# A second layer norm's weights loaded earlier, and turned attention probabilities copied by ScalarE, in a fused three-layer kernel on one Trainium2 core

## The reference, cut to what matters

```python
x = layer_norm(ALPHA * x + gdn_mixer(x, ...), ln_g[0, 0], ln_b[0, 0])   # first norm
x = layer_norm(ALPHA * x + swiglu(x, ...),    ln_g[0, 1], ln_b[0, 1])   # second norm
h = s5_mixer(x, ...)       # its tables depend on weights alone, not on x
...
p = softmax(q @ k.T * scale + bias)   # 8 heads, 256 queries, 256 keys
o = p @ v                             # TensorE wants p with the keys on the partitions: p is turned
```

## Time and profile before

| | |
|---|---|
| median of 3 runs | 1318.15 us (1315.19, 1318.15, 1319.48) |
| the profiled execution, its own time | 1316.35 us |
| its span, on which the trace's times lie | 1314.5 us |
| mean granted TensorE clock | 0.992 of full speed |
| PE busy | 1265.9 us, 96% of the span |
| DVE / ACT / POOL busy | 44% / 18% / 8% |
| read from and written to HBM | 274.19 MB and 16.78 MB |

### The profile page before, as it was taken

The page is one execution under the profiler, slowest core; times in us unless marked ns, Lnnn a source line. Parts: engine busy times, 40 slices in busy tenths (PEclk is TensorE's granted clock), DMA queues, the critical chain, the costliest instruction groups (busy, mean ns, idle before and its releaser), DMA issues.

```text
span 1314.5 us, 25628 instructions
## 1 busy us (share of the span) xinstructions
PE 1265.9 (96%) x11215; PEld 935.5 (71%) x11215; DVE 572.5 (44%) x1078; ACT 234.6 (18%) x494; POOL 111.6 (8%) x109
## 2 busy tenths in 40 slices
PE   7999999999999979899999999999999979999997
PEld 6888985899974448447577767776746645999443
DVE  0653644576789746424211110111062274555545
ACT  2461341123110102502001010100021021111000
POOL 1036102400001000000200000000133000000000
PEclk9999999999999989998999999999999999999999
DMA  9954120565754661747999999999997240353530
GB/s 342 355 210 115 46 97 0 116 176 149 190 225 168 140 125 34 263 170 281 382 418 417 406 406 418 415 405 406 376 349 229 73 184 0 129 191 136 195 120 32
DMA packets 119820, 292.09 MB, mean 222 GB/s; under 512 B 6268, under 2 KB 66144, under 8 KB 107456
## 3 DMA queue, kind: packets, MB, share of 16 engines
q1 hardware_dynamic: 107584, 270.29, 56.9%
q0 software_dynamic: 4800, 14.67, 3.7%
q10 hardware_dynamic: 7360, 6.03, 1.5%
HBM read 274.19 MB, written 16.78 MB: 221 GB/s over the span
## 4 chain that ended last, share of the span: by engine, by line
PE 90%; DVE 5%; ACT 2%; DMA 1%; issue 1%; POOL 0%; DVEq 0%; ACTq 0%; POOLq 0%
PE bank L2565 18%; PE bank L2343 11%; PE bank L2015 9%; PE bank L2582 9%; PE bank L2737 8%; PE bank L2775 7%; PE bank L2028 6%; PE bank L2350 4%; PE bank L2500 4%; PE bank L1987 3%; PE bank L2426 2%; PE bank L2159 1%; PE bank L2449 1%; PE bank L2145 1%; PE bank L2199 1%
## 5 line engine op out<-in xcount | busy, mean ns | idle before, releaser
L2565 PE MATMUL bank<-arena 128*32 128x352 f32 x3072 | 234.8, 461 | 1.4 <-DVE arena L1360 0.7
L2565 PEld LDWEIGHTS bank<-arena 128*32 128x32 f32 x3072 | 142.5, 110 | 87.6 <-issue 6.7
L2015 PE MATMUL bank<-xT,arena 128*128 128x256 f32 x608 | 133.8, 379 | 2.2 <-ACT arena L1695 1.4
L2015 PEld LDWEIGHTS bank<-xT,arena 128*128 128x128 f32 x608 | 114.4, 190 | 17.9 <-ACT arena L1695 1.8
L2582 PE MATMUL bank<-arena 128*32 128x256 f32 x2112 | 119.3, 379 | 0.0
L2582 PEld LDWEIGHTS bank<-arena 128*32 128x32 f32 x2112 | 108.0, 110 | 8.9
L1405 DVE TENSOR_TENSOR arena<-arena,bank 128x352 f32<-128x352 f32 x24 | 19.3, 805 | 205.7 <-PE bank L2565 205.7
L2775 PE MATMUL bank<-arena 128*128 128x512 f32 x224 | 96.7, 592 | 0.7 <-DVE arena L1537 0.7
L2343 PE MATMUL bank<-xT,arena 128*128 128x128 f32 x704 | 83.1, 275 | 0.0
L2343 PEld LDWEIGHTS bank<-xT,arena 128*128 128x128 f32 x704 | 80.8, 192 | 1.3 <-issue 1.3
L2775 PEld LDWEIGHTS bank<-arena 128*128 128x128 f32 x224 | 42.3, 190 | 53.6 <-issue 49.5
(11 more groups left out here) (424 smaller groups left out, 1499.7 us busy)
## 6 DMA issues: line engine op xcount, KB each, us to landing
arena<-moe_w SPq DMA_DIRECT2D x64, 1408.0 KB, 14.3
arena<-moe_w SPq DMA_DIRECT2D x24, 1536.0 KB, 16.4
arena<-ffn_w SPq DMA_DIRECT2D x44, 512.0 KB, 6.0
arena<-gdn_w_in SPq DMA_DIRECT2D x8, 2048.0 KB, 20.3
arena<-w_up SPq DMA_DIRECT2D x8, 2048.0 KB, 8.9
arena<-w_down SPq DMA_DIRECT2D x8, 2048.0 KB, 7.7
arena<-ffn_w SPq DMA_DIRECT2D x11, 1024.0 KB, 5.2
slot_rows<-arena SPq DMA_DIRECT2D x1, 9600.0 KB, 50.8
```

What stands on the lines that cost most here:

```text
L2015: last = mm(bank[:, at:at + SEQ], w[:, k, P * m:P * m + P], x[:, k, :], start=(k == 0), stop=(k == KT - 1))
L2565: last = mm(banks[i][32 * q:32 * q + 32, 0:EW1], xg[:, t, EK * s + kk], w[:, kk, EW1 * q:EW1 * q + EW1], start=(s == 0 and kk == 0), stop= ...
```

## The change: what it does

- `norm_w` is scratch no longer. `t_p` is replaced by `t_up`, 1024 words in the arena at 28160, for the first `w_tables`, and by `t_down`, which is `xT` seen flat, for all later tables. `f_c21` moves to the arena at 27136. Both arena pieces lie in the tail of `V`, which only `v_tables(2)` and `v_tables(3)` write.
- POOL no longer waits for `v_ready`; it issues the second norm's two loads right behind the router's weights, ahead of `s5_pool`.
- In the attention the two copies into `probT` leave DVE. ACT makes them (`take_turned`): those of head pair hp stand between the exponentials of steps 2 hp + 2 and 2 hp + 3, the last pair's behind all exponentials. From the second pair on they also wait for the product with the values of the pair before (`pv_done`).

```diff
@@ -243,9 +243,9 @@
         tb = region(34784, PAIRS, GC)
         kzero = region(35296, 1024)
 
-        flat_w = norm_w[:].rearrange("p a b -> p (a b)")
-        t_p, t_v = flat_w[:, 0:PIECE * 9 * GC], flat_w[:, PIECE * 9 * GC:PIECE * 9 * GC * 3 // 2]
-        f_c21 = flat_w[:, 1728:1984].rearrange("p (a b) -> p a b", a=2)
+        t_up = region(28160, PIECE * SUB * GC)
+        t_down = xT[:].rearrange("p a b -> p (a b)")[:, 0:PIECE * 9 * GC]
+        f_c21 = region(27136, 2, P)
         d_col = d_small[0:2 * GC]
 
         s5_in_w = [region(o_, 4, DM) for o_ in (0, 4096)]
@@ -720,10 +720,9 @@
 
             pool.wait_ge(norm_done, 4)
             pool.dma_start(w_router, A["moe_w_router"][0].rearrange("(k p) f -> p k f", p=P)).then_inc(small_loaded, 16)
-            s5_pool(pool, link)
-            pool.wait_ge(v_ready, 2 * NPIECE)
             norm_load(0, "ln_g", DM)
             norm_load(1, "ln_b", DM)
+            s5_pool(pool, link)
             for n in (2, 3):
                 pool.wait_ge(norm_done, 4 * n)
                 norm_load(0, "ln_g", n * DM)
@@ -1116,7 +1115,7 @@
                 if j:
                     dve.wait_ge(w_tr, 4 * j)
                 for part in parts:
-                    s5_w_table(V_, link, j, part, t_p).then_inc(w_ready, 1)
+                    s5_w_table(V_, link, j, part, t_down if j else t_up).then_inc(w_ready, 1)
                     dve.wait_ge(w_ready, 2 * j + part + 1)
 
             def s5_pieces(c):
@@ -1222,7 +1221,7 @@
             def v_tables(j):
 
                 for part in range(2):
-                    s5_v_table(V_, link, slice(PIECE * j, PIECE * (j + 1)), part, t_p).then_inc(v_ready, 1)
+                    s5_v_table(V_, link, slice(PIECE * j, PIECE * (j + 1)), part, t_down).then_inc(v_ready, 1)
                     dve.wait_ge(v_ready, 2 * j + part + 1)
 
             def take_kernel(j):
@@ -1505,10 +1504,6 @@
                 V_.tensor_tensor(p, p, total[:, :, None].broadcast_to((P, 2, SEQ)), ALU.mult).then_inc(pn_ready, 1)
                 if n == 0 and hp:
                     head_outputs(hp - 1)
-                if n == 1:
-                    for kt in range(2):
-                        dve.wait_ge(pt_done, 2 * hp + kt + 1)
-                        V_.tensor_copy(probT[:, kt].rearrange("p a b -> p (a b)"), banks[4 + kt][:, :]).then_inc(pt_read, 1)
             head_outputs(3)
 
             def weight_sums(j):
@@ -1930,15 +1925,26 @@
             for m in range(4):
                 act.wait_ge(p_done, 2 + m + 1)
                 A_(q2[:, m], banks[4 + m][:, 0:SEQ], ACT.Copy, scale=AD ** -0.5).then_inc(p_read_a, 1)
+            def take_turned(hp):
+
+                for kt in range(2):
+                    act.wait_ge(pt_done, 2 * hp + kt + 1)
+                    if hp:
+                        act.wait_ge(pv_done, hp)
+                    nc.scalar.copy(probT[:, kt].rearrange("p a b -> p (a b)"), banks[4 + kt][:, :]).then_inc(pt_read, 1)
+
             for hp in range(4):
                 for n in range(NT):
                     i = 2 * hp + n
+                    if n and hp:
+                        take_turned(hp - 1)
                     act.wait_ge(max_ready, i + 1)
                     if hp >= 2:
                         act.wait_ge(pt_done, 2 * (hp - 1))
                     for e in range(2):
                         A_(prob[hp % 2][:, n, e], banks[2 * n + e][:, 0:SEQ], ACT.Exp, bias=nmax[:, n, e:e + 1],
                            accum_out=psum_p[:, n, e:e + 1]).then_inc(exp_done, 1)
+            take_turned(3)
             for n in range(NT):
                 vector_step()
                 mean_square(n)
```

## The result

Five runs of the changed kernel took 1308.39 to 1311.82 us, median 1310.27; five runs of the kernel before took 1315.19 to 1319.98, median 1319.48. The ratio is 0.9943, with a 95% interval of 0.9931 to 0.9956. On the prediction's base of 1317.25 that is 7.5 us less, about 1309.7, where 9.2 less, 1308.0, was forecast. On the same base the interval stands for 5.8 to 9.1 us less: it holds rival B's 7.2 and just leaves out 9.2. So the kernel is faster and the time lies in the range, but the gain is nearer to B's. The trace says that it is B.

A forecast was written before the change was run, and what follows sets the result against it. PE work was taken as the bound, 90% of the chain that ended last. Second norm 9.0 plus attention 0.2, other costs 0, made 9.2 us off 1317.25: forecast 1308.0 us, range 1305.0 to 1312.5.

The forecast's parts named there:

- rival B: Products up: third chunk's weights come 3.6 us late, PE loses 2.0, gain is 7.2 us (1310.0); chance 0.12.
- Part 1: Second norm: earlier weight loads save 9.0 us, from PE's 6.3 stall plus 0.9 (transposes) and 1.8 (matmuls) at half clock.
- Rival A: Second norm: the wait goes but not the whole stretch, so only about 5.5 us is gained (1311.7); chance 0.10.
- The cost of the earlier loads: Products up: 1 MB added beside the third chunk's weights was taken to cost 0, with 2.0 us kept for the range.
- bound from above: Third chunk's weights: 2.5 us transfer plus 1.1 us later issue on POOL, 3.6 us in all; PE would lose 2.0.
- second step: Products up: DVE's work ends 1.6 us before PE wants it, cover to set against the 3.6 us delay.
- The S5 parameters: POOL's S5 loads, now behind the norm loads: 1.1 or 3.6 us later, inside 5 us of cover before ACT; cost 0.
- Rival C: Small S5 loads land 24 us late, PE stands 19 us, net 10 us slower (1327); chance 0.03.
- The scratch: Tables: scratch in `xT` and the arena instead of `norm_w` changes only the address; cost nothing.
- Part 2: Attention: copies moved from DVE to ACT gain 0 in three middle rounds and 0.2 us in the last.
- Shifted whole: S5 and the experts: all that follows the second norm was let move earlier by its full 9.0 us.
- Rival D: A later stage that waits for data alone swallows all of the 9.2 us (1317); chance 0.03.

The follow-up runs named there:

- e1: Kernel before with only the scratch moved, norm loads still waiting for the tables; S5 input product starts 239.24 us behind the first norm's last turn.
- e2: Kernel before with only ACT's copies of the turned probabilities added; ratio 0.9997 (0.9988 to 1.0005), 12 runs.
- run 150: Not a run's number: 150 packets left in the memset run, the kernel with late norm loads plus an early 1.0 us POOL memset; first sum at +20.92 us.
- a1: The changed kernel run again unaltered; median 1312.44 us of six runs, ratio 0.995 against the kernel before.
- e3: Kernel after with the attention of before, so only scratch and norm loads changed; median 1310.46 us of eight runs, ratio 0.9951.
- e8: Kernel after with POOL's four zero stores moved behind `bb_ready`; third chunk's first sum starts 20.75 us behind the first norm's last turn.
- e9: Kernel after with the two `s_d` loads ahead of the norm loads; third chunk's first sum starts 21.59 us behind the first norm's last turn.

## Why the prediction was right, and where it was not

- **Part 1, 9.0 us: right in sum and in its terms.** With the loads out of everybody's way it is 9.09. Tile 0's turn comes 6.47 us earlier (228.07 behind the first norm's turn before, 221.60 with the loads late) where 6.3 was said, and the clock gives back 2.62 where 0.9 + 1.8 was said. Rival A (5.5 us) is out. That the sum fits to 0.1 us is partly luck: prediction and offset both start from one execution of the kernel before. Against e1 and e2, which keep the wait, the gain with the loads late is 8.6 and 7.7 us (239.24 and 238.35 less 230.65), because the reload landed sooner in them; by the times it is 8.6, with an interval of 7.0 to 10.1.
- **The cost of the earlier loads: the step that failed.** "I take 0" was wrong. The bound from above was what happened: 3.41 us of delay where it said 3.6, and 1.96 us of PE's time (232.61 - 230.65) where it said 2.0. So the gain up to S5 was 7.13 us, rival B's 7.2, to which I had given 0.12. The choice rested on a mean, 2.4 us of DMA time free in ten. But what counts is what is under way when the half goes out. And the two terms of my bound are not the mechanism: it added a transfer of 2.5 us and a later issue of 1.1, while the runs show 2.8 us from the later issue by itself, 3.4 with the bytes in front of it, and 4.4 from the bytes with the list issued on time. So the bound came out near by luck. What held is its second step: 3.41 us less the 1.6 of cover leaves PE 1.8, and 1.96 was measured.
- **The S5 parameters, cost 0: right** for those who use them; ACT never waits. What I left out is what those loads, moved, do to somebody else's transfer. Rival C (24 us late) is out: the `s_d` loads landed 7.1 us after issue, not 6.1.
- **The scratch, 0: right** (e1).
- **Part 2, 0.2 us: right.** Rounds of 6.91 us as before, 0.22 in the last one, by the traces; the times cannot show it.
- **Shifted whole: right, as far as it can be seen.** The input product of S5 starts 5.58 us earlier on the trace's own axis (482.91 to 477.33: 7.13 less the 1.55 by which the turn was late), the attention's scores 5.93 (1050.67 to 1044.74), the output product 6.15 (1080.79 to 1074.64), the end 6.1. Rival D is out.
- **The total.** 9.09 - 1.96 + 0.22 = 7.35 us against the 7.5 of the ratio, whose interval is 5.8 to 9.1; with the scatter of the first term, that they agree to 0.15 is luck too.

## What to carry to other kernels

When a load is moved to a place that looks idle, a mean share of the DMA engines does not price it: find the next transfer on the path, look at what is under way at its issue, and count every DMA that the move pushes next to it, not only the one that is moved. If the data is wanted 200 us later, there is a better place than the first free one; here a place 117 us further on gave the 2 us back. And where a wait leaves PE standing, count the half clock behind it as well: here it was 2.6 us on top of 6.5.

## What was unexpected in the hardware

- A memset of 1 us on POOL, ahead of a list of small loads, delays another queue's load of 512 KB by 2.7 us (7.6 to 10.3) though that load is issued at the same moment; two tiny loads in its place give the same 10.3. The DMA queues in the ten microseconds from +10 on, in the memset run and then with the loads late (packets, MB, share of 16 engines' time; q1 is SP's queue, q0 POOL's):

```profile
q1 hardware_dynamic: 2074, 1.05, 59.6%
q0 software_dynamic: 384, 0.80, 39.1%
```

```profile
q1 hardware_dynamic: 2080, 1.05, 57.6%
q0 software_dynamic: 345, 0.76, 31.0%
```

  SP's packets as a whole take hardly more of the engines' time. What is late is their end. With the loads late all 2080 have been moved by +18. In the memset run 150 are left then; these are the next two microseconds, one by one:

```profile
q1 hardware_dynamic: 73, 0.03, 31.3%
```

```profile
q1 hardware_dynamic: 71, 0.03, 11.7%
```

  31.3% and 11.7% of 16 engines are the time of about five and two engines (an estimate from these shares). So the load's landing waits for the packets of a few DMA engines while most have done their part. Why these few are behind is open.
- In the kernel after SP's packets are slow as a whole: in the same ten microseconds its 1.03 MB took 72.5% of 16 engines' time, where 1.05 MB took 54.4% before (71.5%, 71.0% and 73.4% in a1, e3 and e8). With the `s_d` loads first (e9) it is 59.3%, and the sum is as late as ever, so this slowness is not what the delay needs. The kernel after, then before:

```profile
q1 hardware_dynamic: 2033, 1.03, 72.5%
q0 software_dynamic: 382, 0.80, 36.2%
```

```profile
q1 hardware_dynamic: 2080, 1.05, 54.4%
q0 software_dynamic: 345, 0.76, 31.3%
```

- One and the same pair of 512 KB loads landed 10.6 and 12.43 us after issue beside the tables' loads, 5.2 and 6.3 us beside the S5 loads, and 4.1 and 5.3 in the late place. The Trainium skill, DMA: Bandwidth & Descriptors, section Anatomy of one DMA, gives 2.0 us and a rate of 436 GB/s, from which I estimated 3.2 and 4.4 for the pair; only the late place comes within 1 us of that, and the measured landings decide.
- From S5's input product to the attention's scores the fourteen profiled executions took 566.7 to 570.5 us, though nothing was changed there: the changed kernel alone shows 567.4 and 570.5. So 2 us cannot be read off one execution's span here, and two marks within a stage are the better measure.
